# The last output projection in half by seven block products, and the last norm and its stores in two halves of the tokens

## The reference

```python
v = silu(layernorm(v, cln_g, cln_b))
v = v @ pw2_w + pw2_b                     # 1024 x 1024
y_conv = v * silu(cs)
...
y = jnp.concatenate([y_conv, y_lru], axis=-1) @ w_out      # 2048 x 1024
x = x + (1.0 + gate[:, None, :]) * y
return rmsnorm_2(x, final_g)              # x * rsqrt(mean(x*x) + eps) * final_g
```

## Time and profile before

| | us |
|---|---|
| median of 3 runs (1029.79 to 1030.02) | 1029.87 |
| the profiled execution | 1030.01 |
| its span in the profile | 1028.2 |
| PE busy in the span | 1009.9 (98%) |
| DVE, ACT, POOL busy | 744.7, 509.8, 503.2 |

### The profile page before, as it was taken

One profiled execution on the slowest core, in us unless ns is written; L12 is line 12 of the kernel. 1 busy time (PEld: TensorE's weight loads), 2 busy tenths in 40 slices (PEclk: granted clock), 3 DMA queues, 4 the chain that ended last, 5 costly groups with the idle time before them and its releaser, 6 DMA issues.

```text
span 1028.2 us, 15845 instructions
## 1 busy us (share of the span) xinstructions
PE 1009.9 (98%) x5814; PEld 844.4 (82%) x5814; DVE 744.7 (72%) x1423; ACT 509.8 (50%) x781; POOL 503.2 (49%) x207
## 2 busy tenths in 40 slices
PE   6999999999999999999999999999999999999997
PEld 5687787677888999999978888888887778888886
DVE  6368998786876555655687866699999999885322
ACT  4243324885366565566652224535436877363232
POOL 0034243682355856656445344348855766633440
PEclk9999999999999999999999999999999999999999
DMA  9994222150222342333299842234321322223212
GB/s 322 349 300 145 83 83 82 43 165 2 82 82 83 106 132 91 102 124 100 83 298 298 292 135 82 83 123 122 121 85 57 106 72 94 93 81 114 82 41 82
DMA packets 127385, 128.98 MB, mean 125 GB/s; under 512 B 3680, under 2 KB 125408, under 8 KB 127328
## 3 DMA queue, kind: packets, MB, share of 16 engines
q1 hardware_dynamic: 126080, 127.38, 38.3%
q10 hardware_dynamic: 1248, 0.86, 0.3%
HBM read 126.13 MB, written 2.10 MB: 125 GB/s over the span
## 4 chain that ended last, share of the span: by engine, by line
PE 75%; issue 11%; POOL 9%; SPq 1%; DMA 1%; ACT 1%; DVE 0%; POOLq 0%; DVEq 0%; ACTq 0%
PE bank L826 17%; PE bank L828 16%; PE bank L827 16%; POOL w_a L757 3%; POOL w_hi L757 2%; PE bank L1173 2%; PE bank L1144 2%; PE bank L1016 2%; POOL w_s L766 2%; POOL w_lo L664 2%; PE bank L1465 1%; PE bank L1467 1%; PE bank L1466 1%; PE bank L838 1%; PE bank L840 1%
## 5 line engine op out<-in xcount | busy, mean ns | idle before, releaser
L664 POOL TENSOR_TENSOR w_lo<-w_stage,w_hi 128x2048 fp32r<-128x2048 f32 x58 | 278.0, 4794 | 369.3 <-ACT w_hi L1538 358.3
L826 PE MATMUL bank<-act_hi,w_hi 128*128 128x512 f32 x528 | 209.9, 397 | 0.1
L828 PE MATMUL bank<-act_hi,w_lo 128*128 128x512 f32 x528 | 205.6, 389 | 0.0
L827 PE MATMUL bank<-act_lo,w_hi 128*128 128x512 f32 x528 | 205.5, 389 | 0.0
L1538 ACT ACTIVATE w_hi<-w_stage 128x2048 fp32r<-128x2048 f32 x59 | 112.9, 1913 | 148.2 <-PE bank L828 130.8
L2736 DVE SCALAR_TENSOR_TENSOR bank<-v_pad,vcol,bank 128x512 f32<-128x512 f32 x208 | 138.2, 745 | 0.0
L826 PEld LDWEIGHTS bank<-act_hi,w_hi 128*128 128x128 f32 x528 | 99.1, 188 | 26.2 <-issue 4.9
L827 PEld LDWEIGHTS bank<-act_lo,w_hi 128*128 128x128 f32 x528 | 99.2, 188 | 21.2 <-issue 1.4
L828 PEld LDWEIGHTS bank<-act_hi,w_lo 128*128 128x128 f32 x528 | 99.1, 188 | 21.1
L826 PE MATMUL bank<-ff_hi,w_hi 128*128 128x512 f32 x176 | 70.1, 398 | 1.1 <-POOL w_lo L664 1.1
L828 PE MATMUL bank<-ff_hi,w_lo 128*128 128x512 f32 x176 | 69.3, 394 | 0.0
(11 more groups left out here) (409 smaller groups left out, 2547.3 us busy)
## 6 DMA issues: line engine op xcount, KB each, us to landing
w_stage<-in_w_in SPq DMA_DIRECT2D x29, 1024.0 KB, 5.2
ada_stage<-in_w_ada SPq DMA_DIRECT2D x20, 1024.0 KB, 11.4
w_stage<-in_w_gu SPq DMA_DIRECT2D x14, 1024.0 KB, 5.1
w_stage<-in_w_out SPq DMA_DIRECT2D x12, 1024.0 KB, 5.2
late_stage<-in_mod_w SPq DMA_DIRECT2D x12, 1024.0 KB, 8.8
w_stage<-in_w_gu SPq DMA_DIRECT2D x16, 512.0 KB, 3.6
w_stage<-in_w_down SPq DMA_DIRECT2D x8, 1024.0 KB, 5.6
late_stage<-in_w_ada SPq DMA_DIRECT2D x4, 1024.0 KB, 11.4
```

Source lines behind the costliest of these rows:

```text
L664: nc.gpsimd.tensor_tensor(low[:], w_stage[b][:], high[:].bitcast(F32), ALU.subtract).then_inc(s_lo, 1)
L826: pe.matmul(dst, wh, rhs_hi(k), start=(first and k == 0), stop=False)
L827: pe.matmul(dst, wh, rhs_lo(k), start=False, stop=False)
L828: mm = pe.matmul(dst, wl, rhs_hi(k), start=False, stop=(last and k == n_k - 1))
```

## The change

The eight output tiles of `C_OUT2` are no longer all made alike. The first four stay as they were. The last two chunks (`C_ROUND` and the one behind it, output tiles 4 to 7) become one round of seven block products. The contraction is cut into even and odd feature tiles, the tokens into `low_t` and `high_t` (256 each), the outputs into tiles 4, 5 and 6, 7. Each block product has two halves m (one output tile each) of 12 matmuls of 256 columns. There are no combining sums of products: banks a and b gather several products, and each stage of a bank is added with the gain straight to the part of `xT` that it belongs to (`out_add` 1 to 14, DVE, 256 columns).

For this, sums of the activations are needed. DVE makes them while it takes the tiles of `C_PW2`: per pair of tiles four differences of token halves (`yc_sum`), each with a cast and a low part. The sums of the weights are made by copies of ACT into banks 5 and 6, `out_sum` and `out_sum_lo` of DVE and `out_sum_hi` of ACT; POOL makes five low parts and differences of 128x1024 in place of two low parts of 128x2048.

The last norm goes by token halves: the squares of tiles 4 to 7 are taken by halves; the sums of the low half stand between the two halves of the last product, the transposes of tokens 0 to 127 behind it, then the sums of the high half. Roots, reciprocals, scalings and stores follow by 128 tokens.

The diff, cut (declarations of buffers and constants, `sum_half` and `by_token` as well):

```diff
@@ POOL
-            lo_loop(first_y + KD - 1, C_END)
+            lo_loop(first_y + KD - 1, C_ROUND)
+            for q, (dst, ks) in enumerate(((o_a11, even_k), (o_a12, odd_k))):
+                pool.wait_ge(s_bhi, PART_END + q + 1)
+                block_lo(dst, w_stage[b_gate][:, ks, :])
...
@@ PE
-            for t in range(KD):
-                residual_tile(C_OUT2, t, hi, lo,
-                              lambda t: pe.wait_ge(*((s_yc, 4 + 4 + t + 1) if t < 4 else (s_res, 3 * KD + t - 3))),
-                              lambda k: pe.wait_ge(s_yclo, k + 1))
+            for t in range(4):
+                residual_tile(C_OUT2, t, hi, lo, lambda t: pe.wait_ge(s_yc, 4 + 4 + t + 1), lambda k: pe.wait_ge(s_yclo, 2 * k + 1))
...
+            pe.wait_ge(s_blo, PART_LO_END + 1)
+            for m in range(2):
+                pe.wait_ge(s_res, 3 * KD + m + 1)
+                product(o_a[m], o_a11, m, o_b11, True)
+            pe.wait_ge(s_blo, PART_LO_END + 2)
+            for m in range(2):
+                product(o_c[m], o_a12, m, o_b21, True)
+            pe.wait_ge(s_yclo, YC_SUMS)
+            for m in range(2):
+                pe.wait_ge(s_slo, LO_END + 1 + m)
+                pe.wait_ge(s_res, 3 * KD + 3 + m)
+                product(o_b[m], w_s1, m, o_t1, True)
+            for m in range(2):
+                pe.wait_ge(s_slo, LO_END + 3 + m)
+                pe.wait_ge(s_cv, CV_END + 1 + m)
+                product(o_a[m], w_s2, m, o_t2, False)
+            pe.wait_ge(s_blo, PART_LO_END + 3)
+            for m in range(2):
+                pe.wait_ge(s_cv, CV_END + 7 + m)
+                product(o_a[m], w_s3, m, o_t3, False)
+            pe.wait_ge(s_blo, PART_LO_END + 4)
+            for m in range(2):
+                pe.wait_ge(s_cv, CV_END + 9 + m)
+                product(o_a[m], w_a22, m, o_t4, False)
+            for m in range(2):
+                pe.wait_ge(s_slo, LO_END + 5 + m)
+                product(o_b[m], o_s4, m, o_b22, False)
+                if m == 0:
+                    pe.wait_ge(s_sqused, SQ_ADDED + 8)
+                    sum_half(5, rstd, 0, True, False)
+                    pe.wait_ge(s_sq, SQ_DONE + 10)
+                    sum_half(5, tmp[2], 0, False, True).then_inc(s_col, 1)
+
+            pe.wait_ge(s_xg, 10)
+            pe.wait_ge(s_cv, CV_END + 12)
+            by_token(0)
...
+            by_token(3)
@@ ACT
-            squares(last_tile, behind=times_gain)
...
+            def out_sum_hi(i, m):
+
+                act.wait_ge(s_sadd, SUM_END + YC_SUMS + 2 * i + m + 1)
+                nc.scalar.activation(o_sums[i][:, low_k, m * P:(m + 1) * P], bank_v[m][:].rearrange("p (k c) -> p k c", k=HK),
+                                     ACT.Copy).then_inc(s_shi, 1)
...
@@ DVE
+            def yc_part(dst_hi, dst_lo, src, hi_done):
+
+                V.tensor_copy(dst_hi, src).then_inc(s_ychi, 1)
+                dve.wait_ge(s_ychi, hi_done)
+                V.tensor_tensor(dst_lo, src, dst_hi.bitcast(F32), ALU.subtract).then_inc(s_yclo, 1)
+
             for k in range(KD):
+                j, y = k // 2, tmp[k % 2]
+                at = SUM_END + 4 * j
...
+                yc_part(act_hi[:, k, :], act_lo[:, k, :], y[:], 2 * k + 1)
+                if k % 2 == 0:
+                    operand_sum(yc_sum[:, 0, :], y[:, high_t], y[:, low_t], ALU.subtract)
+                    dve.wait_ge(s_sadd, at + 1)
+                    yc_part(yc_sum_hi[:, 0, j, :], yc_sum_lo[:, 0, j, :], yc_sum[:, 0, :], 2 * k + 2)
+                else:
+                    operand_sum(yc_sum[:, 1, :], y[:, high_t], tmp[0][:, high_t], ALU.subtract)
+                    operand_sum(yc_sum[:, 2, :], y[:, high_t], yc_sum[:, 0, :], ALU.subtract)
+                    dve.wait_ge(s_sadd, at + 3)
+                    operand_sum(yc_sum[:, 3, :], y[:, low_t], yc_sum[:, 2, :], ALU.subtract)
+                    dve.wait_ge(s_sadd, at + 4)
+                    yc_part(yc_sum_hi[:, 1:4, j, :], yc_sum_lo[:, 1:4, j, :], yc_sum[:, 1:4, :], 2 * k + 2)
...
+            def out_add(n):
...
+                V.scalar_tensor_tensor(xT[:, t, ts], bank[OUT_BANKS[m][b]][:, 0:HT], scale1[:, 3, t:t + 1], xT[:, t, ts],
+                                       ALU.mult, ALU.add).then_inc(s_cv, 1)
```

More of the change, by code:

```diff
@@ L51 @@
 C_OUT2 = C_PW2 + 4
-C_END = C_OUT2 + 4
+C_ROUND = C_OUT2 + 2
+C_END = C_ROUND + 2
 ADA1, ADA2 = 24, 12
@@ L874, in sums @@
                     return mm
[L876 to L879, removed]
+                plain = 2 if gained else 6
                 if before:
@@ new lines, in _, with sum_half @@
+            o_b11, o_b21, o_b22 = [(act_hi[:, ks, ts], act_lo[:, ks, ts]) for ks, ts in ((even_k, low_t), (odd_k, low_t), (odd_k, high_t))]
+            o_t1, o_t3, o_t2, o_t4 = [(yc_sum_hi[:, i, :, :], yc_sum_lo[:, i, :, :]) for i in range(4)]
+            o_a, o_b, o_c = [[bank[OUT_BANKS[m][i]][:, 0:HT] for m in range(2)] for i in range(3)]
+            def sum_half(b, src, half, opens, closes):
+                for t in (2 * half, 2 * half + 1):
+                    mm = pe.matmul(bank[b][:, t * P:(t + 1) * P], src[:, t * P:(t + 1) * P], ones[:],
+                                   start=(opens and t == 2 * half), stop=closes, skip_group_check=True)
+                return mm
@@ new lines, in _ @@
+            gained(3)
+            for m in range(2):
+                out_sum_hi(2, m)
+            for q in range(4):
+                half_square(q)
+                half_gained(q)
+            half_square(4)
+            half_square(5)
+            half_gained(4)
+            half_gained(5)
+            half_square(6)
+            act.wait_ge(s_col, 4)
+            nc.scalar.activation(cols[:, 4, 0:2], first_of_block(bank[5])[:, 0:2], ACT.Sqrt, bias=eps[:, 0:1], scale=1.0 / D).then_inc(s_sd, 1)
@@ new lines, in _ @@
+            residual_2(C_OUT2, 3 * KD, 0)
+            residual_2(C_OUT2, 3 * KD, 1)
+            add_square(1)
+            out_sum(0, 0)
+            out_sum(0, 1)
+            residual_2(C_OUT2, 3 * KD, 2)
+            for i in range(2):
+                for m in range(2):
+                    out_sum_lo(i, m)
+                if i == 0:
+                    for m in range(2):
+                        out_sum(1, m)
+            residual_2(C_OUT2, 3 * KD, 3)
+            for m in range(2):
+                out_sum(2, m)
@@ new lines, in _ @@
+            out_add(1)
+            out_add(2)
+            for m in range(2):
+                out_sum_lo(2, m)
+            out_add(3)
+            out_add(4)
+            add_square(2)
+            add_square(3)
+            out_add(5)
+            out_add(6)
+            out_add(7)
+            out_add(8)
+            add_square(4)
+            out_add(9)
+            add_square(5)
+            out_add(10)
+            out_add(11)
+            add_square(6)
+            add_square(7)
+            out_add(12)
```

213 lines of the change are left out of this document (145 added, 68 removed).

## The result

The changed kernel takes 1032.43 us (median of 11 runs, 1031.54 to 1032.91), the kernel before 1029.99 in the runs beside it (1029.52 to 1031.49). The ratio is 1.002, with a 95% interval of 1.0011 to 1.0029: slower by 0.2%. The forecast was 1028.7, its range ended at 1031.2. The profiled execution took 1031.73 us.

The account below looks back on a forecast made before the run. PE, busy 98% of the span, was taken to bound the kernel, with what follows its last matmul. Terms -2.27 + 0.88 - 3.26 + 0.13 + 3.25 = -1.27 us gave 1028.7 us against a median of 1029.87; range 1025.0 to 1031.2.

Parts of the forecast that it names:

- The round: PE, last four tiles of `C_OUT2`: 168 matmuls of 256 columns replace 96 of 512, 19.50 for 21.77 us, -2.27.
- the sums: PE, between the halves of the last product: 8 matmuls of column sums, +0.88 us.
- the way to the first store: From PE's last product to the first store: 1.75 us instead of 5.01, -3.26.
- the stores: End of the program: transfer flow still sets the end, 7.9 us for 7.77, +0.13.
- The stall: First tile of `C_OUT2`: PE waits for tile 7's `act_lo`, whose cast POOL's low part holds; +3.25 us, range 3.0 to 3.6.
- the rest of it ... to 971.2; then tile 6, 3.0, to 974.2. POOL asks again at 974.11 and gets in there: DVE finishes tile 5's work at 971.2 and tile 6's at 974.2, so POOL's next low part catches tile 7's cast.
- rival B: Behind PE's stall the clock also drops to half rate, +2.7 us more, 1031.4 us, slower; chance 0.14.
- Rival A: No stall: DVE keeps the port through short pauses and POOL's low parts move back; 1025.5 us; chance 0.27.
- Rival C: DVE 2.1 us later, tile 6's cast caught too; PE loses 6.4 us instead of 3.25; 1031.9 us, slower; chance 0.12.

Follow-up runs that it names:

- The first experiment: Changed kernel with POOL's last whole low part made to wait until after tile 7's `act_lo`: 1026.13 us; repeated on another chip, 1025.79 us.
- experiment 3: Changed kernel with 19 extra matmuls of 512 columns keeping PE busy where it waits for tile 7: 1030.14 us.
- experiment 2: Changed kernel with tile 7's three DVE operations placed ahead of tile 6's sum in the last pair: 1030.10 us.
- experiment 4: Changed kernel with POOL's last whole low part cut into four instructions of a quarter: 1030.59 us.
- experiments 5 and 9: Changed kernel's tail alone, without round or activation sums: all four last tiles in 256-token blocks, 1030.16 us; only tile 7 in two halves, 1029.61 us.

## Why the prediction was wrong

*The round, the sums, the way to the first store, the stores.* Right. Forecast -2.27, +0.88, -3.26 and +0.13, measured -1.97 (19.80 for 21.77), +0.81, -3.25 and +0.09. The round ran at 0.118 us for a matmul, between the two pitches of the earlier trace rows and nearer to the slow one than the round of the earlier trace rows, where I took the mean. Together -4.3 for -4.5. The first experiment shows it whole: with 0.28 us of the stall left the kernel takes 1026.1 and 1025.8 us, where the parts without a stall had made 1025.5.

*The stall.* The mechanism was right: PE's place, the releaser and the culprit are those of the forecast. The size was not, 4.54 for 3.25, because the cast that POOL caught was not tile 7's but that of tile 6's sum. The step that failed is "the rest of it ... to 971.2; then tile 6, 3.0, to 974.2. POOL asks again at 974.11 and gets in there". DVE came to tile 6 at 971.82. 0.39 of these 0.6 us are the cast of 768 columns, 0.95 us for the 0.56 that I had estimated with a bound of 0.65: the bound extended the shorter casts' rate and did not ask whether the new shape keeps it. 0.2 is POOL's instruction before, which itself waited for a DVE operation (4.84 for 4.61, issued at 962.94). So at 974.08 POOL met DVE three operations further back in its order, and the cast and the low part of tile 6's sum and the product of tile 7, 1.3 us, came behind the release and not ahead of it. I had called the shift sharp, 3.0 to 3.6; it steps by the length of whatever operation stands there.

*The clock.* This is the step that took the time out of my range. I left its price out of the forecast, put it at nothing in the sum, and gave rival B 0.14. With the stall as long as it was but the clock at 1.00, experiment 3 took 1030.14 us, inside 1025.0 to 1031.2; the changed kernel took 1032.43. In the profiled executions the clock fell in all three versions with a stall that leaves PE idle (the changed kernel, experiments 2 and 4), and in none where PE worked (1 and 3). Experiment 2 has nearly the stall that I forecast, 3.08 us, and there the clock fell too, by the times in most of its runs and probably not in three of eleven. So B was no rival to the forecast but a likely consequence of it: the row that I had, a fall some 3.1 us after PE's last work, spoke of just the idle time that I predicted. Its price, taken as +2.7, is above the 1.4 to 2.3 us of experiment 3. With a price of 1.4 to 2.3 the forecast would have been 1030.1 to 1031.0, and the stall's missing 1.3 brings that to 1031.4 to 1032.3. That experiment 2 measured 1030.10 bears it out only roughly, as its runs spread over 3.5 us.

*Rival A* falls: POOL's last two low parts took 4.84 and 4.57 us, so neither waited for more than part of one DVE operation. *Rival C* (tile 6 caught as well) came half true: tile 6's sum was caught, its `act_lo` was not.

*The sum:* -4.3 for the parts meant, +4.54 of stall and +1.48 of clock make +1.7, against -1.3 forecast; the misses are 1.3 of stall, 1.5 of clock and 0.2 of the rest. Between the medians the change is +2.44; the 0.7 us more is not in the profiled execution, and its cause stays open.

## What to carry to other kernels

Where two engines shut each other out, add both engines' work of a stretch, not each one's share, and ask which operation stands at the moment the other asks: here a wait on POOL, whose result PE reads nearly 10 us after POOL could have begun it, was worth 6 us. A stall forecast for PE has to be priced with the clock that may fall in it, as one case. And the price of a new shape on DVE comes from a row of the same layout, not from its number of elements.

## What the runs showed of the hardware that I had not expected

- A cast of 768 fp32 columns took 0.95 us into three pieces of 256 and 0.56 into one piece, from the same source.
- Cutting POOL's instruction in four did not free DVE: one or two operations between two quarters, four of five held, by 0.3 to 1.1 us each, `act_lo` 1.1 us sooner and POOL 0.8 us longer (5.39 for 4.57).
- The clock fell when PE had been idle for 3.9 us in the changed kernel (976.8 to about 980.7) and for 2.7 in experiment 4; in experiment 2 it fell 0.25 us after PE had gone on from an idle time of 2.9. It came back 3.0, 3.7 and 6.2 us after PE had gone on. These are three executions; by the times of the other runs the price of the same wait differs from one to the next.
- 256-column matmuls stood 0.120 us apart in experiments 5 and 9 and 0.118 in the round, where half of a 512-column one is 0.113: splitting a tile into halves of the tokens costs 6% here.
